# Trainium2 kernel: first level of a blocked triangular inverse built by VectorE from the masked matrix

## What is computed

```
lower = where(strict, einsum(kb, k) * decay, 0.0)          # 64 x 64 per chunk and head
rhs = concatenate([v * beta, kb * exp(gc)])
sol = triangular_solve(lower, rhs, lower=True, unit_diagonal=True)
u, w = sol[..., :dv], sol[..., dv:]
...
v_new = u_n - w_n @ state                                  # then a scan over the chunks
```

## Time and profile before

| what | value |
|---|---|
| median of 3 runs | 2633.23 us (2628.09 to 2636.66) |
| profiled execution | 2635.63 us |
| its span, first to last instruction | 2633.8 us |
| mean granted TensorE clock | 0.981 |
| PE busy, share of the span | 96% |
| DVE, ACT, POOL busy | 59%, 40%, 37% |

### The profile page before, as it was taken

The page is one execution under the profiler, slowest core; times in us unless marked ns, Lnnn a source line. Parts: engine busy times, 40 slices in busy tenths (PEclk is TensorE's granted clock), DMA queues, the critical chain, the costliest instruction groups (busy, mean ns, idle before and its releaser), DMA issues.

```text
span 2633.8 us, 36663 instructions
## 1 busy us (share of the span) xinstructions
PE 2525.4 (96%) x14406; PEld 2000.4 (76%) x14406; DVE 1541.9 (59%) x1966; ACT 1058.7 (40%) x1624; POOL 972.7 (37%) x258
## 2 busy tenths in 40 slices
PE   8999889999999899999989999999999999899998
PEld 7777847888887678888867777787557787688886
DVE  6736654645436756442364779995765787644244
ACT  5444453322223554222244355562654553432222
POOL 0346723444443114444443333332003563244443
PEclk9999989999999999999999999999999999899999
DMA  5224512222222102222233333335443332122222
GB/s 186 96 81 172 183 49 96 100 96 96 96 96 99 49 18 99 101 98 99 97 110 112 116 112 120 120 131 165 116 134 108 133 134 99 65 97 98 100 99 86
DMA packets 72394, 280.61 MB, mean 107 GB/s; under 512 B 10019, under 2 KB 27645, under 8 KB 45123
## 3 DMA queue, kind: packets, MB, share of 16 engines
q1 hardware_dynamic: 59875, 259.72, 28.6%
q10 hardware_dynamic: 12384, 18.99, 1.9%
HBM read 259.21 MB, written 19.40 MB: 106 GB/s over the span
## 4 chain that ended last, share of the span: by engine, by line
PE 70%; issue 16%; DVE 6%; POOL 4%; ACT 3%; DMA 0%; POOLq 0%; DVEq 0%; ACTq 0%
PE banks L610 15%; PE banks L612 15%; PE banks L611 15%; POOL w_lo L3434 4%; PE banks L1073 2%; PE banks L1074 2%; PE banks L1075 2%; PE banks L2802 2%; PE banks L1979 1%; PE banks L2914 1%; PE banks L2915 1%; PE banks L2916 1%; PE banks L2770 1%; PE banks L2546 1%; PE banks L2825 1%
## 5 line engine op out<-in xcount | busy, mean ns | idle before, releaser
L3434 POOL TENSOR_TENSOR w_lo<-raw,w_hi 128x2048 fp32r<-128x2048 f32 x162 | 746.5, 4608 | 1319.0 <-ACT w_hi L588 1261.0
L610 PE MATMUL banks<-hn_hi,w_hi 128*128 128x512 f32 x1896 | 746.3, 394 | 15.5 <-DVE hn_lo L2295 7.8
L611 PE MATMUL banks<-hn_lo,w_hi 128*128 128x512 f32 x1896 | 740.3, 390 | 0.0
L612 PE MATMUL banks<-hn_hi,w_lo 128*128 128x512 f32 x1896 | 740.1, 390 | 0.0
L588 ACT ACTIVATE w_hi<-raw 128x2048 fp32r<-128x2048 f32 x180 | 345.0, 1916 | 575.4 <-PE banks L612 473.0
L610 PEld LDWEIGHTS banks<-hn_hi,w_hi 128*128 128x128 f32 x1896 | 357.4, 189 | 106.1 <-issue 24.0
L612 PEld LDWEIGHTS banks<-hn_hi,w_lo 128*128 128x128 f32 x1896 | 357.2, 188 | 75.3
L611 PEld LDWEIGHTS banks<-hn_lo,w_hi 128*128 128x128 f32 x1896 | 357.7, 189 | 73.3 <-issue 0.2
L1011 DVE TENSOR_TENSOR hid_lo<-prod,hid_hi 128x512 f32 x62 | 280.6, 4526 | 119.0 <-ACT hid_hi L973 119.0
L1008 DVE TENSOR_TENSOR prod<-sg,banks 128x512 f32<-128x512 f32 x62 | 42.6, 687 | 233.4 <-PE banks L612 233.4
L610 PE MATMUL banks<-hid_hi,w_hi 128*128 128x512 f32 x416 | 163.2, 392 | 3.6 <-POOL w_lo L3434 2.2
(11 more groups left out here) (580 smaller groups left out, 3990.9 us busy)
## 6 DMA issues: line engine op xcount, KB each, us to landing
raw<-in_W SPq DMA_DIRECT2D x202, 1024.0 KB, 4.8
oh_early<-codes SPq DMA_DIRECT2D x88, 128.0 KB, 2.8
extra<-in_W SPq DMA_DIRECT2D x8, 1024.0 KB, 4.8
spill<-cs ACTq DMA_DIRECT2D x32, 256.0 KB, 4.4
spill<-mem_q ACTq DMA_DIRECT2D x32, 256.0 KB, 3.3
oh_late<-codes SPq DMA_DIRECT2D x40, 128.0 KB, 2.7
grp<-spill SPq DMA_DIRECT2D x8, 512.0 KB, 4.5
grp<-spill SPq DMA_DIRECT2D x16, 256.0 KB, 4.9
```

The lines of the kernel that those rows point to most:

```text
L610: pe.matmul(out, wh, xh(k), start=(k == 0), stop=False)
L611: pe.matmul(out, wh, xl(k), start=False, stop=False)
L612: mm = pe.matmul(out, wl, xh(k), start=False, stop=(k == nkt - 1))
L3434: pool.tensor_tensor(w_lo[:, u % 2, :], raw[:, u % 2, :], w_hi[:, u % 2, :].bitcast(F32), ALU.subtract).then_inc(S("w_lo"), 1)
```

## The change

At level 0, DVE now makes X transposed directly: it masks `lt` with the transposed mask M_0 (two instructions, one for each half of the partitions, L1956) and subtracts the result from the identity (L1959). These three run for head h - 1 after the four multiplications of head h, and for the last head at the end (`dve_first_level`). PE still has a first round at level 0, but it now only turns `xb` into `xi` by a product with the identity (L1978), and DVE copies that out of PSUM (L2028). The masking of level 0 and the whole second round of level 0 (`iw`, `iv` and their subtractions) are gone, and their banks leave the plan. The semaphore `taps` gets the name `gdn_step` and is counted on by the new instructions.

```diff
-              for x in ([x] if x == "iz" else ["iw", "iv"]) if not (x == "iw" and lv == 6)], range(8))
+              for x in ([x] if x == "iz" else ["iw", "iv"]) if not (x == "iw" and lv == 6) and (lv or x == "iz")], range(8))
...
                 v.tensor_tensor(qkv[:, h, :], qkv[:, h, :], bank(key)[:, :], ALU.mult).then_inc(reads(key), 1)
+                if h:
+                    dve_first_level(v, h - 1)
+            dve_first_level(v, HG - 1)
+
+        def dve_first_level(v, h):
+            eye = levels[:, 6:7, :].broadcast_to([P, NC, 64])
+            taken(v, ("kk", h))
+            for b_, half in enumerate(HALF):
+                v.tensor_tensor(xb[half, h, :, :], chunked(lt[half, h, :])[:, :, 64 * b_:64 * b_ + 64],
+                                levels[half, 0:1, :].broadcast_to([64, NC, 64]), ALU.mult).then_inc(S("gdn_step"), 1)
+            v.wait_ge(S("gdn_step"), 36 + 3 * h + 2)
+            v.tensor_tensor(xb[:, h, :, :], eye, xb[:, h, :, :], ALU.subtract).then_inc(S("gdn_step"), 1)
...
-                    taken(pe, ("iw", lv - 1, h) if lv else ("kk", h))
+                    if lv:
+                        taken(pe, ("iw", lv - 1, h) if lv > 1 else ("iz", 0, h))
+                    else:
+                        pe.wait_ge(S("gdn_step"), 36 + 3 * h + 3)
...
-                            mm = pe.matmul(bank(key)[half, c * 64:c * 64 + 64], corner(lt, h, c, b_),
+                            mm = pe.matmul(bank(key)[half, c * 64:c * 64 + 64], corner(lt, h, c, b_) if lv else xb[half, h, c, :],
...
-                for h in range(HG):
+                for h in range(HG) if lv else ():
...
-            for lv in range(6):
+            for h in range(HG):
+                key = ("iz", 0, h)
+                full(v, key)
+                v.tensor_copy(xi[:, h, :, :], blocks(key)).then_inc(reads(key), 1)
+            for lv in range(1, 6):
```

More of the change, by code:

```diff
@@ L1818, in dve_qkv @@
                         if d > 1:
-                            v.wait_ge(S("taps"), 2 * j + d - 1)
+                            v.wait_ge(S("gdn_step"), 2 * j + d - 1)
                         ins = v.scalar_tensor_tensor(
@@ L1822, in dve_qkv @@
                             in1=qkv[:, j, d:T], op0=ALU.mult, op1=ALU.add)
-                        ins.then_inc(S("taps") if d < 3 else reads(key), 1)
+                        ins.then_inc(S("gdn_step") if d < 3 else reads(key), 1)
                 if i == 1:
@@ L1966, in pe_inverse @@
                     mm.then_inc(fills(key), 1)
-                for h in range(HG):
+                for h in range(HG) if lv else ():
                     taken(pe, ("iz", lv, h))
-                    if lv:
+                    if lv > 1:
                         taken(pe, ("iv", lv - 1, h))
@@ L1975, in pe_inverse @@
                             for b_, half in enumerate(HALF):
-                                xtc = xb[half, h, c, :] if lv else ident[half, half]
+                                xtc = xb[half, h, c, :]
                                 z_ = zm[half, h, c, :]
@@ L2005, in dve_inverse @@
         def dve_inverse(v):
-            eye = levels[:, 6:7, :].broadcast_to([P, NC, 64])
             low, high = HALF
@@ L2019, in dve_inverse @@
                     full(v, key)
-                    v.tensor_tensor(xi[:, h, :, :], xi[:, h, :, :] if lv else eye, blocks(key), ALU.subtract)\
+                    v.tensor_tensor(xi[:, h, :, :], xi[:, h, :, :], blocks(key), ALU.subtract)\
                         .then_inc(reads(key), 1)
@@ L2024, in dve_inverse @@
                     if lv < 5:
-                        v.tensor_tensor(xb[:, h, :, :], xb[:, h, :, :] if lv else eye, blocks(key), ALU.subtract)\
+                        v.tensor_tensor(xb[:, h, :, :], xb[:, h, :, :], blocks(key), ALU.subtract)\
                             .then_inc(reads(key), 1)
@@ L3757, in layout @@
     s64, c64 = s % 64, np.arange(64)[None, :]
-    a["levels"] = np.stack([((s64 >> lv) % 2 == 1) & ((s64 >> lv) - 1 == (c64 >> lv)) for lv in range(6)]
+    below = [((s64 >> lv) % 2 == 1) & ((s64 >> lv) - 1 == (c64 >> lv)) for lv in range(1, 6)]
+    a["levels"] = np.stack([(c64 % 2 == 1) & (c64 - 1 == s64)] + below
                            + [s64 == c64], 1).astype(BF)
```

## The result

| kernel | median us | lowest to highest | runs |
|---|---|---|---|
| before | 2630.66 | 2627.01 to 2636.66 | 4 |
| changed | 2643.92 | 2642.50 to 2645.92 | 4 |

The account below looks back on a forecast made before the run. PE and DVE, handing work to each other, were taken as the path. New DVE instructions waiting for POOL shift level 1's second round by +21.5 us, nothing given back: profiled 2635.6 becomes 2657, median 2655, range 2640 to 2663 (own range 2650 to 2660).

Parts of the forecast that it names:

- The removed round and the free sets: Level 0's second round saves 5.6 us; unhindered, three new DVE instructions a head make DVE 3.63 us against PE's 2.85.
- the marker: Start of level 1's second round on PE, same lists in both kernels from there; forecast 269.6 against 248.1, +21.5 us.
- Two operands in SBUF wait for POOL, and the two alternate one for one: New DVE instructions meeting POOL's running add wait for its end, then alternate with POOL: 4.7 us per DVE instruction.
- The course: Heads through level 1: sets of heads 0, 1, 3 run free, others meet POOL's adds; last set ends at 264.4.
- The copy of unit 8: POOL's short copy behind its adds holds DVE's last new instruction for 1.91 us; otherwise end 1.8 earlier or 2.6 later.
- The cold groups: After PE's standstill, its seven groups before level 1's second round take 5.1 us at reduced clock; warm 3.3, half clock 6.5.
- Nothing hides or gives back the shift later: Behind level 1's second round the whole +21.5 us stays to the end: the profiled execution of 2635.6 becomes 2657.
- the prediction's own sign: At the recurrence: forecast is wrong if it starts less than 17 us later than before (ACT's copy at 316.88).
- the first rival: DVE keeps the way once it has it, a set waits once: +2.7 us (2636), or 2640 with one add between; chance 0.15.
- the new instructions did have to wait for what POOL holds: Second rival, denying this for the new DVE instructions (bf16 mask, half the partitions): -3.0 us, 2630; chance 0.06.
- no set more was caught: Third rival, claiming one set more (head 1's or 3's) meets POOL's add: +4.7 us, 2660; chance 0.07.

Follow-up runs that it names:

- quiet: Changed kernel with ACT's scaling of units 2 and 3 held until all 18 new DVE instructions are done, so POOL is silent; 2630.16 us, ratio 1.0008.
- small: Kernel before with each side-stream load from unit 3 on cut to 64 of its 2048 columns, so it computes less; 2614.93 us, ratio 0.9938.
- sets: Changed kernel with the new instructions' same elements in six instructions, three heads at a time; 2641.95 us, ratio 1.0063.
- small_after: Changed kernel with each side-stream load from unit 3 on cut to 64 of its 2048 columns, so it computes less; 2639.51 us, ratio 1.0037.
- late: Kernel before with one more wait: PE starts the inverse only when POOL has done unit 7; 2651.94 us, ratio 1.0094.
- pool: Changed kernel with the new first-level instructions made by POOL between its units 1 and 2 instead of by DVE; 2631.17 us, ratio 1.0016.
- split: The kernel of both with each side-stream load from unit 3 on in two halves, the second issued when the first has landed; 2638.11 us, ratio 1.0036.
- both: The kernel of pool, its first level not waiting for ACT's scaling of unit 2, and ACT's units 18 and 19 moved into the recurrence; 2621.05 us, ratio 0.9967.

## Why the prediction was right, and where it was not

- **The removed round and the free sets** (5.6 saved, 3.6 us a head against 2.85, -3.0 in all): right. quiet shows it alone, with the marker at -3.0. Of this 1.2 is the pause that before makes ahead of the marker; against small, which has none, quiet gains 1.6 there.
- **Two operands in SBUF wait for POOL, and the two alternate one for one**: right. quiet takes POOL away, and 24.8 us go; sets takes a third of the instructions, and the price of one stays.
- **The course**: right to 0.4 us, mostly to the tenth. Head 2's set was forecast at 230.2 and came at 229.90; the first instruction of head 3's at 236.55 (236.40), head 4's at 240.2 (240.17), POOL's unit 3 at 238.65 (238.72), the sets' end at 264.4 (264.17), the marker at 269.6 (269.58). Seven instructions were long, as forecast.
- **The copy of unit 8**, on which the trace of before was silent: DVE's last instruction started at 262.17, behind the copy of 261.80 to 263.89, and ended at 264.17. It waited for the copy at the copy's own length, the value that was taken.
- **The cold groups** (5.1 us for seven): 264.32 to 269.58 is 5.26. PE's granted clock was 0.50 over 242 to 264 and 1.00 over 270 to 318, as these windows of the changed kernel show, which also answer:

```profile
242.00:264.00 22.00, 2.51 (x43) 2.16 (x40) 21.87 (x6) 8.43 (x5) 21.32 (x6) 0.50 0.60 203
270.00:318.00 48.00, 43.34 (x1389) 42.43 (x1386) 38.63 (x94) 18.04 (x9) 41.44 (x10) 1.00 0.70 242
```

- **"Nothing hides or gives back the shift later"**: wrong by the traces, and by the prediction's own sign: the recurrence was to start at least 17 us later, and ACT's copy of 316.88 came at 327.45, 10.6 later (10.9 from the common start). The time of 2643.92 lies in the stated range, but outside the 2650 to 2660 that the forecast gave itself; it fell into the part that had been taken in for the first rival, which the same trace refutes. That much was luck. Of the 11.1 us between 2655 and the median, 2.6 is that the median of before came out at 2630.66 and not 2633.23, and 8.2 is that the medians differ by 13.3 and not by 21.5. The levels were read as a pair of engines that hand work to each other; 10.6 us in them belonged to neither, and stood in the list of waits as "issue". In the changed kernel 4.6 of the 10.6 are left, which with 1.3 of other work is the 7.3 given back. small and small_after show that the pauses need the loads. Why fewer came is argued, not shown. One part may be a full buffer: while PE stood still it used up no instructions, and its first pause came at 283.90, 14 us behind the marker. late (4.3 us of pauses) fits this, but pool's PE had stood for 4.3 us only and paused 3.5, and sets' PE had stood for 13.4 and paused 12.6. The records of q8 show a larger part: in before eleven fetches serve the levels, from 247.79 to 296.99, 4.9 us apart, and in the changed kernel eleven, from 268.58 to 313.08, 4.5 apart. Over ten intervals that is 4.7 us, of the 6.0 by which the pauses shrank. In both traces of before, in quiet, sets, split and both traces of both, one fetch of the levels or more comes only 5.9 to 6.7 us after the last, mostly with a pause of 1.6 to 2.8 us behind it; in the changed kernel, late and pool no interval is over 5.0. So how the fetches fall among the loads seems to count for more than the standstill; no run set it on purpose.
- **The rest of the way back**: from the last level to the recurrence 3.7 us, and from there to the end 2.7 to 3.6 (7.3 + 3.7 + 3.6 is 14.6, the distance between the forecast's 2657 for a profiled execution and the 2642.5 that came). Both parts go with PE's granted clock. From the last level to the recurrence it was 0.75 in before and 1.00 in the changed kernel:

```profile
303.47:316.88 13.41, 12.27 (x105) 11.62 (x103) 9.85 (x20) 0.00 (x0) 4.97 (x2) 0.75 0.45 159
```

```profile
317.70:327.45 9.75, 8.88 (x105) 8.39 (x103) 9.69 (x22) 0.00 (x1) 0.00 (x0) 1.00 0.01 3
```

  Summed from the records of the granted clock, PE stood at the lower level for 6.8, 3.4 and 0 us of this stretch in before, its second trace and the changed kernel, which took 13.4, 11.6 and 9.7. From the recurrence to the end it was 84.7, 81.4 and 74.9 us, for 2316.9, 2316.0 and 2313.3. The two traces of both, one and the same kernel, have 88.3 and 67.7 us there, and 2319.2 and 2313.2. So this part differs between executions by more than what is to be explained, and it can't be put down to the change. Why the changed kernel, sets, late and small_after all lie low there (71 to 75 us) stays open.
- **The rivals** fell by the same rows: DVE did not keep the way, the new instructions did have to wait for what POOL holds, and no set more was caught.

## What to carry to other kernels

An instruction that VectorE takes from SBUF alone costs one instruction of GpSimd, here 4.6 us instead of 0.42, whenever GpSimd has its own queued without a break: count instructions, not elements, and give such work to GpSimd itself if it is idle for a while. Before a delay is carried through to the end of a program, read the "issue" waits of the engine behind it: time that belongs to no engine's work can shrink, or grow, when the delay comes. Keep the time of each stage apart from the granted clock in it, since two executions of one kernel can differ there by 6 us. And a large transfer that runs beside many small products may cost TensorE its instructions, though none of them reads what the transfer brings.

## What the runs showed of the hardware

- TensorE waits for its own instructions: 10.4 to 12.6 us of pauses in 55 to 58 us of 64x64 products beside 1 MB loads, one every 4.7 us (before, quiet, sets), 3.5 to 9.1 in the changed kernel, late, pool and both, and 0.2 us with 32 KB loads. The Trainium skill, "Runtime: NRT & Kernel Launch", section "Instruction fetch mechanics", calls the cost of fetching mostly hidden; in this case the measurement disagrees, and decides.
- The same section of the Trainium skill gives PE a buffer of 2048 instructions. After a standstill of 10.2 us PE ran from 264.32 to its first pause at 283.90 with 1200 instructions on record (588 products, 612 of the weight-load queue), 4.7 fetches' worth at 256 each by estimate. Four were fetched in that time, as the queue's line of 264.4 to 283.9 shows; the fourth ended at 283.33, and the pause ended 1.4 us after it, so three had come in time. By this PE had between one and two blocks of 256 at hand, not eight. A note in that section of the Trainium skill speaks of two blocks of 16 KB, and the trace agrees with that one.

```profile
q8 instruction: 4, 0.07, 1.3%
```

- A mask in bf16 and half the partitions do not free a VectorE instruction from the wait for GpSimd: 64x256 took 4.0 to 4.7 on average in pairs.
